# First block: VectorE takes the modulation rows and the attention step between the heads' sums of squares and the heads' scaling and finish

## The chip, the cores and the metric

The program runs on one core of a Trainium2 chip. The metric is the device time of one launch in microseconds (us), the median of the timed runs. The engines are named as in the profile: PE (TensorE), DVE (VectorE), ACT (ScalarE), POOL (GpSimd), and SP, whose queue carries the weight transfers.

## The reference, cut to what matters

Two transformer-like blocks run one after the other on 256 tokens of width 1024. The change touches the input projections of the first block, which has two layers:

```python
for l in range(DEPTH):                       # DEPTH = 2
    sh, sc, gt = jnp.split(jax.nn.silu(c) @ w_ada[l] + b_ada[l], 3, axis=-1)   # modulation rows; also for c_ctx
    h  = rms_norm(x, norm_g[l]) * (1 + sc[:, None]) + sh[:, None]
    hc = rms_norm(ctx, norm_g[l]) * (1 + sc_c) + sh_c
    qa, ka, va, ga, qb, kb, vb, gb, qn, kn, vn, gn = split_proj(h @ w_in[l])   # and the same of hc
    qa = axial_rope(rms_norm(qa.reshape(b, s, A_HEADS, 2, A_DK), diff_q_norm[l]), row, col)   # "heads": per-head
    qn = rms_norm(qn.reshape(b, s, C_HEADS, HEAD_DIM), nat_q_norm[l])                         # norm, some with rope
    ...
    oa = ...  (p[:, :, 0] - lam * p[:, :, 1]) @ v      # A: differential attention, 4 heads
    yb = gqa_attend(qb, kb_all, vb_all)                # B: grouped queries, 6 heads
    yn = neighbourhood_attend(qn, kn, ...)             # C: windowed attention with a bias table, 6 heads
    x = x + gt[:, None] * (jnp.concatenate([ya, yb, yn], axis=-1) @ w_out[l])
```

The change alters the order of some VectorE instructions and no value that is computed.

## The kernel before, in words

Tokens and context make four tiles of 128 rows (two of tokens, two of context). A projection is a run of chunks of 512 output columns; a chunk is four pieces, and a piece is two of the eight 128-row blocks of the contraction. The input projection of layer 0 is called in0, that of layer 1 in1; each has seven chunks. Below, (c, n) is piece n of chunk c.

Each weight piece is loaded by the SP queue into one of three raw buffers, split by ACT into a high part (L1093) and by DVE into a low part (L1685), and multiplied by PE three times (L739 to L741). In in0 DVE also works through the modulation weights beside each piece: four products (L1702, L1705) of one modulation piece. When four are done, PE sums them over the partitions (L666 for the column form, L673 for the gate rows) into bank 6 (gate rows: banks 6 and 7), and DVE adds the bias and stores them: `ada_keep`, L1713 and L1719 for columns, L1726 for gate rows. That falls at (2,0), (3,0), (4,0), (5,0) and (6,0) of in0. Layer 1's projection has no such work.

The heads of chunks 0, 2, 4 and 5 are normalised one chunk later, beside the pieces of the next chunk, so in chunks 1, 3, 5 and 6. At piece n the loop calls `process_in` with stage n + 2: ACT squares the heads of tile n + 2 (L1194), DVE sums the squares (`sum_squares`, L1822), POOL makes the reciprocal root (L1493, L1495), DVE scales tile n + 1 (`scale`, L1830), and DVE applies gain and rope to tile n (`finish`, L1848, L1853), for which POOL makes the rope's second product (L519). Tiles 0 and 1 are summed, and tile 0 is scaled, at the end of the chunk before. PE then turns a finished tile (L759): tile 0 in the middle and tile 1 at the end of piece 2, tile 2 in the middle and tile 3 at the end of piece 3.

From (2,1) on, one step of attention runs beside each piece. On PE a step is: the scores of the next unit, or of the next two (L863), the turn of the probabilities of the unit before (L873, into bank 6), and the attention product of the one before that (L888, into bank 7). On ACT: copy the turned probabilities (L1282), exponentials (L1273), for A heads a sum of squares of the output (L1293). On DVE: maxima of the new scores (L1901), weights of the current unit (L1912 to L1918, or L1926), and the output (L1936).

All engines run their instructions strictly in the order in which the program issues them and wait on semaphores. A bank of PSUM is taken again only when its last user has released it: bank 6 passes from modulation sums to turned probabilities when `ada_keep` has read it, the score banks 4 and 5 when the exponentials have read them. The order on DVE beside a piece was: heads (sum, scale, finish), `ada_keep`, attention step, the low part of the piece four ahead (L1685), modulation products. The next transfer of a weight piece waits until L1685 has read its raw buffer.

Of the kernel before, what the change touches and what calls it, by code (L numbers as in the profile page):

```python
# [64 lines left out]
def tiles_of(ph):  # L65
    return ALL_TILES if ph in ("in0", "out0", "in1") else X_TILES
# [164 lines left out]
def first_then_second_block(nc, a, out, known):  # L231
# [11 lines left out]
    with ExitStack() as ctx:  # L243
# [256 lines left out]
        for layer in range(2):  # L500
            n = 0
# [1176 lines left out]
        def _(dve):  # L1678
            at = [0]

            def split_until(n):
                for i in range(at[0], min(n, len(SPLITS))):
                    p = SPLITS[i]
                    dve.wait_ge(*weights_hi.seen(p))
                    dve.tensor_tensor(w_lo[:, i % SPLIT, :, :], raw[:, PIECE_AT[p] % RAW, :, :],  # L1685
                                      w_hi[:, i % SPLIT, :, :].bitcast(F32), ALU.subtract).then_inc(*weights_lo.at(p))
                at[0] = max(at[0], n)
# [97 lines left out]
            def project(ph, process, after_piece=None):  # L1785
                pairs = PROJ[ph][1] // 2
                limit = SPLIT_AT[(ph, 0, 0)] + PROJ[ph][0] * pairs if ph == "in0" else len(SPLITS)
                for c in range(PROJ[ph][0] - (1 if FOLLOWING.get(ph) and pairs <= SPLIT else 0)):
                    for n in range(pairs):
                        p = (ph, c, n)  # L1790
                        if ph in FOLLOWING and c == PROJ[ph][0] - 1 and n >= pairs - SPLIT:
                            continue
                        if after_piece:
                            after_piece((p, 0))
                        if ph in ("in0", "in1"):
                            process(ph, c - 1, (n + 2,))
                        if p in ADA_READY:
                            ada_keep(*ADA_READY[p])
                        if after_piece:
                            after_piece((p, 1))  # L1800
                        if n < pairs - 1:
                            split_until(min(limit, SPLIT_AT[p] + SPLIT + 1))
                        if p in ADA_BESIDE:
                            ada_products(ADA_BESIDE[p])
                        if n == pairs - 1:
                            split_until(min(limit, SPLIT_AT[p] + SPLIT + (1 if ph in FOLLOWING else 0)))
                            process(ph, c)
                            split_until(min(limit, SPLIT_AT[p] + SPLIT + 1))

            def process_in(ph, c, stages=(0, 1)):  # L1810


                if c not in CHUNK_HEADS:
# [4 lines left out]
                def sum_squares(tt):  # L1818
                    u = (ph, c, tt)
                    lo, w = head_span(*u)  # L1820
                    dve.wait_ge(*head_sq.seen(u))
                    dve.tensor_reduce(ss_of(tt % 2, w // d), sq[:, lo:lo + w].rearrange("p (n d) -> p n d", d=d), AX, ALU.add) \  # L1822
                        .then_inc(*head_sum.at(u))
# [31 lines left out]

                tts = tiles_of(ph)
                for k in stages:
                    if k < len(tts):
                        sum_squares(tts[k])
                    if 1 <= k <= len(tts):  # L1860
                        scale(tts[k - 1])
                    if k >= 2:
                        finish(tts[k - 2])

            def out_tile(ph, c, tt):
# [184 lines left out]
            project_with("in1", process_in, attention1(1))  # L2050
            y_part("out1", X_TILES[-1], 1)
            project("out1", process_out)
            end_of("out1", out_tile)

# [183 lines left out]
```

## Time and profile before

| | us |
|---|---|
| timed runs, median of 3 | 1259.74 |
| lowest and highest | 1258.07, 1260.96 |
| profiled execution, its own time | 1252.77 |
| its span | 1250.9 |
| PE busy in the span | 1137.0 (91%) |
| DVE busy | 727.0 (58%) |
| ACT busy | 598.6 (48%) |
| POOL busy | 256.8 (21%) |

The trace is of the profiled execution, whose time lies 7 us under the median of the timed ones; 1.9 us of it lie outside the span. In0 runs from about 28 to 290 us of the span, in1 from about 435 to 632 us. Times in the rows are microseconds from the start of the span. A row of a timeline merges neighbouring instructions of one kind; its second number runs from the first start to the last end, and in brackets stands the idle time of the engine before it and what ended that.

### The profile page before, as it was taken

What the parts mean: (1) busy time and instruction counts of PE and PEld (TensorE: products, weight loads), DVE (VectorE), ACT (ScalarE), POOL (GpSimd) and SP (SyncE); (2) the same over time, 40 slices, a digit from 0 to 9 for tenths busy, and PEclk for the clock granted to TensorE, in tenths of its full rate; (3) what the DMA queues carried; (4) which work ended last, traced back from release to release, by engine and by line L of the source; (5) the groups of instructions that cost most, each with busy time, mean ns of one, the idle gap of its engine ahead of it and who ended that gap; (6) DMA issues with size and microseconds to landing.
All of it is one profiled execution on the core that took longest, in us unless ns stands there. A gap on an engine that the chain in (4) does not pass through costs nothing.

```text
span 1250.9 us, 16717 instructions
## 1 busy us (share of the span) xinstructions
PE 1137.0 (91%) x5877; PEld 905.5 (72%) x5877; DVE 727.0 (58%) x1330; ACT 598.6 (48%) x1170; POOL 256.8 (21%) x324
## 2 busy tenths in 40 slices
PE   5978799898989878999989898999699999999997
PEld 2666578676668766777867686888588887888785
DVE  3467777777763744644455666565566646565543
ACT  3433453435762444554474454445444455454552
POOL 1482330354005221302300203000122101121100
PEclk8989899899999998899999899999999999999999
DMA  9755364323122322222202765555356665444301
GB/s 333 146 160 183 102 148 135 113 90 122 48 68 73 100 68 84 68 71 82 71 32 68 264 199 160 157 175 180 126 178 182 185 186 151 121 131 119 118 2 51
DMA packets 79290, 157.94 MB, mean 126 GB/s; under 512 B 5792, under 2 KB 6088, under 8 KB 78952
## 3 DMA queue, kind: packets, MB, share of 16 engines
q1 hardware_dynamic: 75880, 147.41, 38.0%
q0 software_dynamic: 3328, 9.46, 3.3%
q8 instruction: 49, 0.80, 0.3%
q14 instruction: 33, 0.27, 0.1%
HBM read 153.73 MB, written 3.11 MB: 125 GB/s over the span
## 4 chain that ended last, share of the span: by engine, by line
PE 71%; DVE 11%; ACT 6%; POOL 5%; issue 4%; DMA 2%; SPq 0%; ACTq 0%; POOLq 0%; DVEq 0%
PE bank L739 17%; PE bank L741 16%; PE bank L740 16%; PE bank L888 5%; PE bank L863 3%; PE bank L873 3%; POOL small L1495 3%; PE bank L966 2%; DVE work L1705 2%; DVE w_lo L1685 2%; PE bank L939 2%; PE bank L951 2%; ACT w_hi L1093 1%; PE bank L759 1%; POOL stage L519 1%
## 5 line engine op out<-in xcount | busy, mean ns | idle before, releaser
L739 PE MATMUL bank<-w_lo,h_hi 128*128 128x512 f32 (+1 forms) x1152 | 462.3, 401 | 27.7 <-DVE h_lo L1754 11.8
L741 PE MATMUL bank<-w_hi,h_hi 128*128 128x512 f32 (+1 forms) x1152 | 447.5, 388 | 0.0
L740 PE MATMUL bank<-w_hi,h_lo 128*128 128x512 f32 (+1 forms) x1152 | 447.1, 388 | 0.0
L1685 DVE TENSOR_TENSOR w_lo<-raw,w_hi 128x1024 fp32r<-128x1024 f32 x224 | 286.7, 1286 | 176.0 <-ACT w_hi L1093 174.5
L1093 ACT ACTIVATE w_hi<-raw 128x1024 fp32r<-128x1024 f32 x224 | 235.8, 1057 | 277.4 <-PE bank L741 237.8
L739 PEld LDWEIGHTS bank<-w_lo,h_hi 128*128 128x128 f32 x1152 | 222.6, 193 | 77.7 <-issue 29.7
L741 PEld LDWEIGHTS bank<-w_hi,h_hi 128*128 128x128 f32 x1152 | 221.7, 192 | 44.9
L740 PEld LDWEIGHTS bank<-w_hi,h_lo 128*128 128x128 f32 x1152 | 222.7, 193 | 39.5 <-issue 0.2
L888 PE MATMUL bank<-work,stage 128*128 128x128 f32 x640 | 94.4, 290 | 0.0
L1673 POOL TENSOR_TENSOR stage<-stage 128x512 f32<-128x512 f32 x24 | 42.3, 1784 | 218.0 <-DVE stage L519 218.0
L888 PEld LDWEIGHTS bank<-work,stage 128*128 128x128 f32 x640 | 85.5, 205 | 1.0 <-issue 0.2
L1282 ACT ACTIVATE stage<-bank 128x512 f32<-128x512 f32 (+1 forms) x96 | 50.2, 523 | 72.1 <-PE bank L873 71.9
L873 PEld LDWEIGHTS bank<-ident,stage 128*128 128x128 f32 x320 | 37.0, 147 | 65.3 <-issue 48.5
L1901 DVE TENSOR_REDUCE small<-bank 128x1 f32<-128x512 f32 (+1 forms) x96 | 53.2, 573 | 51.1 <-PE bank L863 51.1
L873 PE MATMUL bank<-ident,stage 128*128 128x128 f32 x320 | 56.9, 295 | 27.3 <-DVE work L1726 8.0
L1493 POOL TENSOR_SCALAR small<-small 128x1 f32<-128x1 f32 (+4 forms) x56 | 21.6, 386 | 268.1 <-DVE small L1822 222.7
L1495 POOL TENSOR_TENSOR small<-small 128x1 f32<-128x1 f32 (+4 forms) x56 | 73.3, 1308 | 4.7
L863 PE MATMUL bank<-work 64*128 64x512 f32 (+3 forms) x240 | 65.0, 582 | 8.6 <-ACT stage L1273 8.6
L1705 DVE SCALAR_TENSOR_TENSOR work<-raw,cvec,work 128x512 f32<-128x512 f32 x98 | 71.7, 781 | 1.2 <-DMA raw<-in_w_ada_dram 0.9
L1936 DVE SCALAR_TENSOR_TENSOR work<-bank,small,work 128x64 f32<-128x64 f32 x96 | 27.0, 282 | 70.8 <-PE bank L888 48.0
L1273 ACT ACTIVATE stage<-bank,small 128x512 f32<-128x512 f32 (+1 forms) x96 | 56.8, 596 | 19.8 <-DVE small L1901 19.5
L1210 ACT ACTIVATE work<-bank 128x512 f32<-128x512 f32 (+2 forms) x56 | 29.9, 534 | 55.8 <-PE bank L759 55.7
(173 smaller groups left out, 1090.7 us busy)
## 6 DMA issues: line engine op xcount, KB each, us to landing
raw<-in_b_w_in_dram SPq DMA_DIRECT2D x80, 512.0 KB, 3.7
raw<-in_w_in_dram SPq DMA_DIRECT2D x56, 512.0 KB, 4.1
raw<-in_a_w_in_dram SPq DMA_DIRECT2D x48, 512.0 KB, 4.3
raw<-in_w_ada_dram SPq DMA_DIRECT2D x32, 512.0 KB, 3.7
work<-in_w_ada_dram SPq DMA_DIRECT2D x16, 512.0 KB, 11.4
raw<-in_w_out_dram SPq DMA_DIRECT2D x16, 512.0 KB, 3.5
raw<-in_a_w_out_dram SPq DMA_DIRECT2D x16, 512.0 KB, 3.6
raw<-in_b_w_out_dram SPq DMA_DIRECT2D x8, 512.0 KB, 3.5
```

The costliest lines, as they stand in the source:

```text
L739: pe.matmul(bank, hT(h_hi, ph, at, tt), w_lo[:, s, k, lo:lo + w], start=first, stop=False)
L740: pe.matmul(bank, hT(h_lo, ph, at, tt), w_hi[:, s, k, lo:lo + w], start=False, stop=False)
L741: mm = pe.matmul(bank, hT(h_hi, ph, at, tt), w_hi[:, s, k, lo:lo + w], start=False, stop=last)
L863: mm = pe.matmul(bank[:, k0:512], qkT[base:base + d, tq, qt * P:(qt + 1) * P], qkT[base:base + d, tk, k0:512], start=True, stop=True)
L873: mm = pe.transpose(bank[:, j * P:(j + 1) * P], probs[prob_slot(layer, u, 0)][:, j * P:(j + 1) * P], ident[:, :])
L888: mm = pe.matmul(bank[:, 0:P], pT[i % 2][:, j * P:(j + 1) * P], vals[:, j, vcol:vcol + P], start=(j == kt0), stop=(j == 3))
L1093: act.activation(w_hi[:, i % SPLIT, :, :], raw[:, PIECE_AT[p] % RAW, :, :], ACT.Copy) \
L1273: act.activation(probs[slot][:, k0:512], bank[:, k0:512], ACT.Exp, bias=nm_col(u, m), accum_out=zc[0]).then_inc(*exps.at((layer, n)))
L1495: pool.tensor_tensor(out_ap, out_ap, half.broadcast_to([P, n]), ALU.pow).then_inc(*done.at(key))
L1685: dve.tensor_tensor(w_lo[:, i % SPLIT, :, :], raw[:, PIECE_AT[p] % RAW, :, :], w_hi[:, i % SPLIT, :, :].bitcast(F32), ALU.subtract).then_i ...
L1705: dve.scalar_tensor_tensor(to, w, c, to, ALU.mult, ALU.add).then_inc(*ada_vector.at((*p, k, who)))
L1901: dve.tensor_reduce(nm_col(u, m), bank[:, k0:512], AX, ALU.max, negate=True).then_inc(*row_max.at((u, m)))
```

## The change

At pieces 0 to 2 of chunks 1, 3, 5 and 6 of in0 and in1, DVE now does only the heads' sums of squares before `ada_keep` and the attention step, and the heads' scaling and finish after them, ahead of the low part of the next piece. At piece 3 of a chunk the order is as before. In chunk 1 there is neither a step nor an `ada_keep`, so nothing moves there. Nine places in each projection change their order. PE, ACT, POOL and SP issue the same instructions in the same order.

```diff
                         if after_piece:
                             after_piece((p, 0))
-                        if ph in ("in0", "in1"):
-                            process(ph, c - 1, (n + 2,))
+                        first_block = ph in ("in0", "in1")
+                        if first_block:
+                            process(ph, c - 1, (n + 2,), ("sum",) if n < pairs - 1 else ("sum", "finish"))
                         if p in ADA_READY:
                             ada_keep(*ADA_READY[p])
                         if after_piece:
                             after_piece((p, 1))
+                        if first_block and n < pairs - 1:
+                            process(ph, c - 1, (n + 2,), ("finish",))
                         if n < pairs - 1:
                             split_until(min(limit, SPLIT_AT[p] + SPLIT + 1))
...
-            def process_in(ph, c, stages=(0, 1)):
+            def process_in(ph, c, stages=(0, 1), parts=("sum", "finish")):
...
                 for k in stages:
-                    if k < len(tts):
+                    if k < len(tts) and "sum" in parts:
                         sum_squares(tts[k])
-                    if 1 <= k <= len(tts):
+                    if 1 <= k <= len(tts) and "finish" in parts:
                         scale(tts[k - 1])
-                    if k >= 2:
+                    if k >= 2 and "finish" in parts:
                         finish(tts[k - 2])
```

DVE at (3,0) of in0, before the change: the heads' sum (L1822), scale (L1830) and finish (L1848, L1853), then the two gate rows (L1726), then the attention step (L1901 to L1936).

```order
L1822 TENSOR_REDUCE small<-stage 128x8
L1830 TENSOR_TENSOR stage<-stage,small 128x512
L1848 TENSOR_TENSOR stage<-stage,tabs 128x384
L1848 TENSOR_TENSOR stage<-stage,tabs 128x128
L1853 TENSOR_TENSOR stage<-stage 128x512
L1726 TENSOR_TENSOR work<-work,bank 128x512 x2
L1901 TENSOR_REDUCE small<-bank 128x1 x2
L1912 RECIPROCAL small<-small 128x2
L1915 TENSOR_SCALAR small<-small 128x1
L1918 SCALAR_TENSOR_TENSOR stage<-stage,small 128x512
L1936 SCALAR_TENSOR_TENSOR work<-bank,small,work 128x64
L1685 TENSOR_TENSOR w_lo<-raw,w_hi 128x1024
```

The same place with the change (lines from L1811 on are numbered 3 higher in it, so L1825 is the sum, L1833 the scale, L1851 and L1856 the finish, L1904 to L1939 the step).

```order
L1825 TENSOR_REDUCE small<-stage 128x8
L1726 TENSOR_TENSOR work<-work,bank 128x512 x2
L1904 TENSOR_REDUCE small<-bank 128x1 x2
L1915 RECIPROCAL small<-small 128x2
L1918 TENSOR_SCALAR small<-small 128x1
L1921 SCALAR_TENSOR_TENSOR stage<-stage,small 128x512
L1939 SCALAR_TENSOR_TENSOR work<-bank,small,work 128x64
L1833 TENSOR_TENSOR stage<-stage,small 128x512
L1851 TENSOR_TENSOR stage<-stage,tabs 128x384
L1851 TENSOR_TENSOR stage<-stage,tabs 128x128
L1856 TENSOR_TENSOR stage<-stage 128x512
L1685 TENSOR_TENSOR w_lo<-raw,w_hi 128x1024
```

The four instructions of scale and finish have gone from ahead of the gate rows and the step to behind them. At (5,0) and (6,0) it is the same with L1713 (and L1719) in the place of L1726.

DVE at (3,0) of in1 with the change, where there are no modulation rows: the maxima of the scores now follow the heads' sum at once.

```order
L1825 TENSOR_REDUCE small<-stage 128x2
L1904 TENSOR_REDUCE small<-bank 128x1 x2
L1915 RECIPROCAL small<-small 128x2
L1918 TENSOR_SCALAR small<-small 128x1
L1921 SCALAR_TENSOR_TENSOR stage<-stage,small 128x512
L1939 SCALAR_TENSOR_TENSOR work<-bank,small,work 128x64
L1833 TENSOR_TENSOR stage<-stage,small 128x512
L1851 TENSOR_TENSOR stage<-stage,tabs 128x384
L1851 TENSOR_TENSOR stage<-stage,tabs 128x128
L1856 TENSOR_TENSOR stage<-stage 128x512
```

Before, the last four of these rows stood between the first and the second.

## Rows read from the trace of the kernel before

**Rows 1.** The page, busy time and share of the span by engine.

```profile
PE 1137.0 (91%) x5877; PEld 905.5 (72%) x5877; DVE 727.0 (58%) x1330; ACT 598.6 (48%) x1170; POOL 256.8 (21%) x324
```

**Rows 2.** Waits of PE, 130 to 640 us: total, times, longest.

```profile
PE bank L863 <- ACT stage L1273: 6.4, 4, 2.5
...
PE bank L873 <- DVE ada_cols L1713: 5.2, 2, 4.0
```

**Rows 3.** Timeline of PE in in0: start, length, work, idle before.

```profile
142.62 1.13 PE L863 MATMUL bank<-work 32*128 32x512 f32 x4
150.54 1.09 PE L873 MATMUL bank<-ident,stage 128*128 128x128 f32 x4 [6.79 <-DVE work L1726]
...
178.04 0.66 PE L759 MATMUL bank<-ident,stage 128*128 128x128 f32 x4 [0.30 <-DVE stage L1848]
```

**Rows 4.** Timeline of DVE at (3,0) of in0.

```profile
144.32 0.68 DVE L1822 TENSOR_REDUCE small<-stage 128x8 f32<-128x512 f32 x1
147.71 0.69 DVE L1830 TENSOR_TENSOR stage<-stage,small 128x512 f32<-128x512 f32 x1 [2.71 <-POOL small L1495]
...
149.71 1.28 DVE L1726 TENSOR_TENSOR work<-work,bank 128x512 f32<-128x512 f32 x2
...
153.98 0.28 DVE L1936 SCALAR_TENSOR_TENSOR work<-bank,small,work 128x64 f32<-128x64 f32 x1 [0.63 <-ACT bank L1293]
```

**Rows 5.** Waits of DVE, 144 to 178 us (chunk 3 of in0).

```profile
DVE work L1936 <- ACT bank L1293: 1.9, 3, 0.8
DVE small L1901 <- PE bank L863: 1.7, 2, 1.0
```

**Rows 6.** Windows: PE, PEld, DVE, ACT, POOL busy, granted clock, DMA.

```profile
144.00:146.00 2.00, 0.00 (x0) 0.00 (x0) 1.00 (x2) 0.00 (x0) 1.87 (x3) 0.86 0.28 23
```

**Rows 7.** Timeline of DVE at (5,0) of in0.

```profile
223.33 0.68 DVE L1822 TENSOR_REDUCE small<-stage 128x8 f32<-128x512 f32 x1
...
226.23 0.15 DVE L1713 TENSOR_TENSOR ada_cols<-bank,cols 128x8 f32<-128x8 f32 x1
```

**Rows 8.** Waits of DVE, 223 to 251 us (chunk 5 of in0).

```profile
DVE work L1936 <- ACT bank L1293: 2.5, 3, 1.2
DVE small L1901 <- PE bank L863: 1.7, 2, 1.2
DVE stage L1830 <- POOL small L1495: 0.9, 1, 0.9
```

**Rows 9.** Timeline of POOL, the bias mask of layer 0.

```profile
269.03 7.71 POOL L1552 TENSOR_TENSOR work<-work,win_mask 128x384 f32<-128x384 f32 x6
```

**Rows 10.** Timeline of DVE beside it, pieces 1 and 2 of chunk 6.

```profile
267.18 0.41 DVE L1830 TENSOR_TENSOR stage<-stage,small 128x256 f32<-128x256 f32 x1
...
275.81 1.21 DVE L1830 TENSOR_TENSOR stage<-stage,small 128x256 f32<-128x256 f32 x1
```

**Rows 11.** Timeline of DVE in chunk 3 of in1.

```profile
517.33 0.28 DVE L1822 TENSOR_REDUCE small<-stage 128x2 f32<-128x128 f32 x1
520.73 0.69 DVE L1830 TENSOR_TENSOR stage<-stage,small 128x512 f32<-128x512 f32 x1 [3.12 <-POOL small L1495]
...
522.74 1.28 DVE L1901 TENSOR_REDUCE small<-bank 128x1 f32<-128x512 f32 x2
...
536.61 1.29 DVE L1901 TENSOR_REDUCE small<-bank 128x1 f32<-128x512 f32 x2 [3.84 <-PE bank L863]
```

**Rows 12.** Timeline of PE in chunk 3 of in1.

```profile
524.28 2.74 PE L863 MATMUL bank<-work 32*128 32x512 f32 x4 [2.46 <-ACT stage L1273]
...
534.92 0.60 PE L759 MATMUL bank<-ident,stage 128*128 128x128 f32 x4
```

**Rows 13.** Windows over the same stretch, columns as in rows 6.

```profile
524.00:526.00 2.00, 1.72 (x4) 0.98 (x4) 1.83 (x6) 2.00 (x8) 1.57 (x3) 0.58 0.01 4
526.00:528.00 2.00, 2.00 (x8) 1.05 (x6) 1.97 (x6) 0.34 (x1) 0.94 (x2) 0.50 0.14 14
528.00:536.00 8.00, 8.00 (x45) 6.90 (x43) 4.60 (x10) 3.75 (x9) 0.39 (x1) 0.80 0.44 129
```

## The prediction

> **What bounds the kernel now.** I read the page first: PE is busy for 1137 us, 91% of the span [rows 1], so what counts is what makes PE wait, and DVE matters where PE waits for it. The second view is the waits of PE over the two stretches that the change touches. They name L873, the turn of the probabilities, waiting for `ada_keep`'s column form L1713 (5.2 us in two places, 4.0 and 1.2) and L863, the scores, waiting for exponentials (6.4 us in four places, the longest 2.5) [rows 2]. The timeline of PE has the largest one: at (3,0) of in0 PE ends its scores at 143.75 (142.62 + 1.13) and stands for 6.79 us until the gate rows L1726 have released bank 6 [rows 3]. The third view is DVE's timeline at that place. DVE ended the sum L1822 at 145.0, then waited 2.71 us for POOL's reciprocal root, then scaled and finished (2.00 us, 147.71 to 149.71), and only then read the bank that PE wanted [rows 4]. So the wait of PE is DVE's queue, and inside it POOL's time. At (5,0) the sum ends at 224.0 and L1713 starts at 226.23 [rows 7]. In in1, at (3,0), the sum ends at 517.6, DVE waits 3.12 us for POOL, and the maxima L1901 start at 522.74; the exponentials that need them hold PE's next scores back by 2.46 us, until 524.28 [rows 11, 12].
>
> The granted clock is the fourth view. In the stretch 144 to 146, with PE at rest since 143.75, it fell from 2.4 to 1.2 GHz (mean 0.86) [rows 6]. Round the stall of in1 it is 0.58, 0.50 and 0.80 of full in stretches of 2, 2 and 8 us [rows 13]. With f the mean, 2(1 - f) of a stretch lies at the lower level: 1.7 + 2.0 + 3.2 = 6.9 us.
>
> **The change, part by part.** No instruction is added or removed; on DVE nine groups in each projection change places. The sum is against the profiled execution, 1252.77 us (span 1250.9 and 1.9 outside).
>
> Chunk 3 of in0. L1726 can start at 145.0. Before, PE went on 0.83 us after L1726's start (149.71 to 150.54), so now at 145.8: the stall is 2.1 instead of 6.8 us, PE gains 4.7. DVE does not gain as much. Gate rows, maxima and weights took 153.98 - 149.71 - 0.63 = 3.64 us, so DVE reaches its output L1936 at 148.6; L1936 needs ACT's sum of squares, which comes a fixed chain after PE goes on (150.54 to 153.98, 3.44), at 149.3. POOL's root was there at 147.7, so scale and finish follow at once and end at 149.3 + 0.2 + 2.0 = 151.5, where before the low part started at 154.2: DVE gains 2.7, just the POOL wait. From there on, the two meet at the turns of the heads. DVE's other waits in this chunk are 1.9 (L1936, three) and 1.7 (L1901, two, for PE's scores) [rows 5]. Because PE is ahead now and scale and finish no longer stand before L1901, the 1.7 goes if the clock is up when (3,1) is multiplied, and none of it goes if PE stays at the lower level as long as before. So DVE finishes tile 3, for which PE waited already at 178.04 [rows 3], by 2.7 to 2.7 + 1.7 + 0.3 = 4.7 us earlier. I take 4.4, since PE now rests 2.1 and not 6.8 us. Bounds: 2.7 and, if the clock gives PE another 1.0 and DVE follows, 5.7.
>
> Chunk 5 of in0. L1713 starts at 224.0 instead of 226.2, PE gains 2.2. DVE's waits here sum to 2.5 + 1.7 + 0.9 = 5.1 [rows 8]; the 0.9 on POOL goes, and of the wait for scores some 0.5, because at (5,1) PE is 2.2 ahead and DVE 0.9. That makes 1.4 at the turn of tile 3. Bounds 0.9 (only the POOL wait) and 2.9 (the 2.2 and clock).
>
> Chunk 6 of in0. PE's wait of 1.2 goes. What covers the moved work is thin: at (6,1) scale and finish (0.41 each, as the row at 267.18) ran before POOL began the bias mask at 269.03; now they stand behind L1936, inside the mask's 7.7 us, where such a scale took 1.21 [rows 9, 10]. Two of them cost DVE 1.6 more, and tile 2 is finished behind (6,2)'s L1936, about when PE wants to turn it. I keep 0.4 of the 1.2. Bounds -0.8 and 1.2.
>
> Chunk 3 of in1. The maxima start at 517.6 instead of 522.74, 5.1 earlier. The exponentials and so PE's release would come at 524.28 - 5.1 = 519.2, before PE asks (521.8), so the 2.46 go whole. With no rest there, the 6.9 us at 1.2 GHz need not come: half of it, 3.4, is given back. That is 5.9. DVE is no bound: at (3,2) it waited 3.84 us for PE's scores [rows 11]. The turn of tile 1, at 534.92 before [rows 12], would be at 529.0; its finish, behind (3,1)'s L1936, I put at 528.4 (maxima at 523.9, 2.7 for the step, 0.2 and 1.4 for scale and finish, 0.2 between them), so it just fits. I take 5.8. Bounds 2.7 (DVE's gain at (3,0), if PE follows DVE) and 6.4.
>
> POOL's root is what this rests on in in1: it came at 520.7, and DVE would want it at 520.3. A rule speaks against the change here: by the Trainium skill, SBUF — State Buffer, section "SBUF: two separate sides", a GpSimd instruction and a DVE instruction with two SBUF inputs lock the port pair that they share, and the later one is blocked for the whole instruction. The trace agrees in kind (1.21 against 0.41 [rows 9, 10]). The root's long instruction now runs beside the weights of the step, one of which has two SBUF inputs, instead of an idle DVE; by the rule the root comes up to one such instruction later, and the sum would be some 0.7 smaller.
>
> Chunks 5 and 6 of in1 (six places): PE waited for none of this before, and the moved heads (0.4 to 1.4 us) are wanted by PE's turns microseconds later: nothing. The low part L1685 comes later by the moved heads wherever DVE did not gain; it is for a piece that PE reaches four pieces on, and the transfer behind it has the same cover: nothing, and if the cover failed, up to 1.3 us at a place.
>
> Sum: 4.4 + 1.4 + 0.4 + 5.8 = 12.0. The profiled execution would take 1240.8. The timed runs lay 7.0 us higher, in no place that this trace shows; I carry the offset over: 1259.7 - 12.0 = 1247.7.
>
> **The rivals.** First, the turns follow DVE: PE gets its banks early but then waits for heads that are finished behind an L1936, so that each chunk gives the lower bound, 2.7 + 0.9 - 0.8 + 2.7 = 5.5: 1254.2. For it: PE waits for tile 3 at 178.04 even now. Against: DVE idles 6.3 us in that chunk, and 3.8 at one place of in1.
>
> Second, the clock helps everywhere: 5.7 + 2.9 + 1.2 + 6.4 = 16.2: 1243.5. For it: shorter rests. Against: the clock fell in 144 to 146, while PE would still rest in the new order until 145.8, and the same holds at (5,0).
>
> Third, the change doesn't do what it says: PE at L873 waited for something else, and the bank was only last by the profile. Then nothing moves: 1259.7. Against: PE goes on within a microsecond of L1726 in one place, and of L1713 in another.
>
> Fourth, slower: heads behind the step. The heads of tiles 1 and 2 are now finished only after an L1936 that itself waits for PE and ACT, in six chunks: twelve turns. A group of heads takes 0.4 to 2.0 us, on average about 1.3. If PE waited that long at all twelve, it would lose 15.6 against the 12.0: 3.6 slower, 1263.3. It decides from about nine or ten waited turns on. Against: my placing of the first four has waits of 0 to 0.5 us.
>
> **How the numbers follow.** Forecast 0.60; turns follow DVE 0.18; clock everywhere 0.10; nothing 0.06; slower 0.06. I call 0.2% (2.5 us) what a measurement can tell. Faster holds the first three, 0.88; same 0.06; slower 0.06. The range reaches from the sum of the upper bounds with half a microsecond of spread, 1243.0, to beyond the first rival, 1256.0; what is left out is mainly the last two cases.
>
> **What would show it.** Right: L873's idle at (3,0) of in0 is 2 us, not 6.8, at (5,0) under 2 and not 4.0; no wait of L1833 (the scale) for POOL at (3,0); in in1 L863 at (3,1) waits for nothing and the clock stays at 1.0 there. At the end of chunk 3 of in0 PE is 4 to 5 us ahead, at the end of in0 about 6, at the end of in1 about 12. Wrong: new waits of L759 for L1851 of over 1 us, a clock that falls in in1's chunk 3 all the same, or gains that are gone by the start of the next phase.

## The result, and the profile after

| | before | with the change |
|---|---|---|
| timed runs, median (us) | 1260.35 (1258.07 to 1261.09, 4 runs) | 1240.52 (1236.3 to 1243.42, 4 runs) |
| ratio, 95% interval | | 0.9846 [0.9825, 0.9867] |
| profiled execution, own time | 1252.77 | 1242.56 |
| its span | 1250.9 | 1240.8 |

The change makes the kernel 1.5% faster: 19.8 us, where 12.0 were forecast and the range ended at 1243.0. The two profiled executions differ by only 10.1 us in span. That of before lay 7.6 us under the median of the timed runs of before in this table (7.0 under that of the first three, which the prediction had); the one with the change lies 2.0 us over its own. So most of what the forecast missed is not in this pair of traces, and the experiments had to find it.

First the busy times of the changed kernel, as in [rows 1].

```profile
PE 1134.9 (91%) x5877; PEld 900.9 (73%) x5877; DVE 729.6 (59%) x1330; ACT 599.3 (48%) x1170; POOL 253.8 (20%) x324
```

Busy times hardly move; what goes is idle time of PE and some slow multiplying. The waits of PE, 130 to 640 us (total, times, longest), answer to [rows 2]:

```profile
PE bank L759 <- DVE stage L1851: 3.2, 5, 1.0
...
PE bank L873 <- DVE work L1726: 3.2, 2, 2.0
PE bank L863 <- ACT stage L1273: 3.1, 2, 2.2
PE bank L873 <- DVE ada_cols L1713: 1.7, 1, 1.7
```

L873 waits 1.7 instead of 5.2 us for the column form, and 3.2 instead of 8.0 for the gate rows. The scores lost two of their four waits, the longest (2.5) and one of 0.8 at the end of in1. New is the first row: five turns of heads wait 3.2 us for a finish that now stands behind the step. Before, L1848 made one turn wait, for 0.3 us [rows 3]; the waits of two other turns for L1853, in in1, are there before and after (5.4 and 5.5 us).

Timeline of PE in in0 (start, length, work, idle before), the answer to [rows 3]; the last two rows are the turns of tiles 2 and 3 of chunk 3:

```profile
144.40 1.13 PE L863 MATMUL bank<-work 32*128 32x512 f32 x4
147.53 0.63 PE L873 MATMUL bank<-ident,stage 128*128 128x128 f32 x4 [2.00 <-DVE work L1726]
...
171.24 0.66 PE L759 MATMUL bank<-ident,stage 128*128 128x128 f32 x4 [0.33 <-DVE stage L1851]
...
175.69 0.66 PE L759 MATMUL bank<-ident,stage 128*128 128x128 f32 x4 [1.03 <-DVE stage L1851]
```

Timeline of DVE at the same place, (3,0) of in0, the answer to [rows 4]:

```profile
146.11 0.68 DVE L1825 TENSOR_REDUCE small<-stage 128x8 f32<-128x512 f32 x1
146.70 1.28 DVE L1726 TENSOR_TENSOR work<-work,bank 128x512 f32<-128x512 f32 x2
...
149.60 0.75 DVE L1921 SCALAR_TENSOR_TENSOR stage<-stage,small 128x512 f32<-128x512 f32 x1
150.51 0.28 DVE L1939 SCALAR_TENSOR_TENSOR work<-bank,small,work 128x64 f32<-128x64 f32 x1 [0.16 <-ACT bank L1293]
150.71 0.68 DVE L1833 TENSOR_TENSOR stage<-stage,small 128x512 f32<-128x512 f32 x1
```

The gate rows start as the sum ends, the 2.71 us wait for POOL is gone (the scale at 150.71 has no bracket), and the output L1939 waits 0.16 us. At (5,0) and in chunk 6, PE's rows are these (the last two are turns of tiles 2 and 3 in chunk 6):

```profile
223.44 0.41 PE L873 MATMUL bank<-ident,stage 128*128 128x128 f32 x2 [1.75 <-DVE ada_cols L1713]
...
248.73 0.66 PE L759 MATMUL bank<-ident,stage 128*128 128x128 f32 x4 [1.04 <-DVE stage L1851]
...
277.19 0.44 PE L759 MATMUL bank<-ident,stage 128*128 128x128 f32 x2 [0.18 <-DVE stage L1851]
...
281.01 0.44 PE L759 MATMUL bank<-ident,stage 128*128 128x128 f32 x2 [0.62 <-DVE stage L1851]
```

In in1, DVE at (3,0) and PE's scores at (3,1) answer to [rows 11, 12], and the window (PE, PEld, DVE, ACT, POOL busy, granted clock, DMA) to [rows 13]:

```profile
513.81 0.28 DVE L1825 TENSOR_REDUCE small<-stage 128x2 f32<-128x128 f32 x1
514.00 1.28 DVE L1904 TENSOR_REDUCE small<-bank 128x1 f32<-128x512 f32 x2
...
517.22 0.69 DVE L1833 TENSOR_TENSOR stage<-stage,small 128x512 f32<-128x512 f32 x1 [0.38 <-POOL small L1495]
```

```profile
518.26 1.13 PE L863 MATMUL bank<-work 32*128 32x512 f32 x4
```

```profile
518.00:526.00 8.00, 8.00 (x53) 6.42 (x54) 7.76 (x16) 4.41 (x10) 4.05 (x6) 1.00 0.21 66
```

The maxima follow the sum at once, the scores wait for nothing, and PE stays at 2.4 GHz through the stretch that ran at means of 0.58, 0.50 and 0.80 before. The four matmuls of the scores take 1.13 us there instead of 2.74.

### The profile page after: what moved, and what is told of

The parts are those of the page before. It is cut to its first block, busy times and chain, and to the rows that moved or that the text cites. A ratio compares the mean times of both kernels' runs of the same rounds, so it can differ in the third digit from the quotient of the medians.

```text
span 1240.8 us, 16717 instructions
## 1 busy us (share of the span) xinstructions
PE 1134.9 (91%) x5877; PEld 900.9 (73%) x5877; DVE 729.6 (59%) x1330; ACT 599.3 (48%) x1170; POOL 253.8 (20%) x324
## 3 DMA queue, kind: packets, MB, share of 16 engines
q1 hardware_dynamic: 75880, 147.41, 37.5%
## 4 chain that ended last, share of the span: by engine, by line
PE 60%; DVE 7%; ACT 5%; issue 3%; POOL 2%; DMA 1%; POOLq 0%; ACTq 0%; DVEq 0%; SPq 0%
PE bank L739 14%; PE bank L741 14%; PE bank L740 14%; PE bank L888 4%; PE bank L966 2%; PE bank L873 2%; PE bank L863 2%; PE bank L939 2%; PE bank L951 2%; ACT w_hi L1093 1%; DVE w_lo L1685 1%; PE bank L759 1%; DVE work L1705 1%; POOL small L1495 1%; PE bank L720 1%
## 5 line engine op out<-in xcount | busy, mean ns | idle before, releaser
L739 PE MATMUL bank<-w_lo,h_hi 128*128 128x512 f32 (+1 forms) x1152 | 462.7, 402 | 27.7 <-DVE h_lo L1754 11.8
L739 PEld LDWEIGHTS bank<-w_lo,h_hi 128*128 128x128 f32 x1152 | 222.3, 193 | 78.3 <-issue 30.6
L888 PE MATMUL bank<-work,stage 128*128 128x128 f32 x640 | 91.3, 283 | 0.0
L1904 DVE TENSOR_REDUCE small<-bank 128x1 f32<-128x512 f32 (+1 forms) x96 | 53.3, 574 | 51.4 <-PE bank L863 51.3
L888 PEld LDWEIGHTS bank<-work,stage 128*128 128x128 f32 x640 | 82.0, 198 | 1.2 <-issue 0.4
L873 PEld LDWEIGHTS bank<-ident,stage 128*128 128x128 f32 x320 | 36.1, 145 | 56.9 <-issue 41.7
L1495 POOL TENSOR_TENSOR small<-small 128x1 f32<-128x1 f32 (+4 forms) x56 | 73.5, 1312 | 4.7
L873 PE MATMUL bank<-ident,stage 128*128 128x128 f32 x320 | 55.3, 288 | 18.7 <-DVE h_lo L1782 6.1
L1493 POOL TENSOR_SCALAR small<-small 128x1 f32<-128x1 f32 (+4 forms) x56 | 16.1, 287 | 259.6 <-DVE small L1825 215.8
L1939 DVE SCALAR_TENSOR_TENSOR work<-bank,small,work 128x64 f32<-128x64 f32 x96 | 27.1, 282 | 71.5 <-PE bank L888 49.4
```

The lines of the kernel that those rows point to most:

```text
L739: pe.matmul(bank, hT(h_hi, ph, at, tt), w_lo[:, s, k, lo:lo + w], start=first, stop=False)
L873: mm = pe.transpose(bank[:, j * P:(j + 1) * P], probs[prob_slot(layer, u, 0)][:, j * P:(j + 1) * P], ident[:, :])
L888: mm = pe.matmul(bank[:, 0:P], pT[i % 2][:, j * P:(j + 1) * P], vals[:, j, vcol:vcol + P], start=(j == kt0), stop=(j == 3))
L1495: pool.tensor_tensor(out_ap, out_ap, half.broadcast_to([P, n]), ALU.pow).then_inc(*done.at(key))
L1904: dve.tensor_reduce(nm_col(u, m), bank[:, k0:512], AX, ALU.max, negate=True).then_inc(*row_max.at((u, m)))
```

## The experiments

All are the kernel before with one rule for the "late" order, that is, scaling and finish behind the step. The core of the edit is this, and the experiments differ in the line that sets `late`; the versions that treat the modulation rows otherwise show their own edit below.

```diff
-                            process(ph, c - 1, (n + 2,))
+                            process(ph, c - 1, (n + 2,), ("sum",) if late else ("sum", "finish"))
...
+                        if late:
+                            process(ph, c - 1, (n + 2,), ("finish",))
```

| kernel | late at | median us (range, runs) | before on the same chip | ratio [95%] |
|---|---|---|---|---|
| change, once more | 18 places | 1241.08 (1238.38 to 1244.25, 6) | 1258.3 | 0.9876 [0.9849, 0.9903] |
| change, a third time | 18 places | 1242.09 (1239.76 to 1244.35, 5) | 1258.47 | 0.9875 [0.9856, 0.9895] |
| before, again | none | 1259.12 (1251.93 to 1260.83, 12) | 1258.3 | 1.0005 [0.9984, 1.0025] |
| in0 only | 9 places | 1251.55 (1248.05 to 1254.16, 12) | 1258.3 | 0.9952 [0.9934, 0.9971] |
| in1 only | 9 places | 1250.12 (1246.15 to 1253.27, 11) | 1258.3 | 0.9941 [0.992, 0.9961] |
| chunk 3 of in0 | 3 places | 1250.28 (1247.47 to 1257.42, 8) | 1259.46 | 0.9941 [0.9918, 0.9965] |
| chunk 6 of in0 | 3 places | 1256.49 (1252.02 to 1259.58, 12) | 1259.46 | 0.998 [0.9966, 0.9994] |
| first places | 4 places | 1239.81 (1237.46 to 1243.08, 4) | 1259.46 | 0.9846 [0.9826, 0.9866] |
| first places, again | 4 places | 1237.75 (1237.35 to 1243.6, 5) | 1258.47 | 0.9852 [0.9827, 0.9877] |
| first places, third | 4 places | 1242.02 (1238.29 to 1243.6, 4) | 1259.63 | 0.9856 [0.9839, 0.9872] |
| modulation rows first | in0, rows alone | 1247.78 (1241.31 to 1250.39, 6) | 1259.46 | 0.9898 [0.987, 0.9927] |
| the same and (3,0) of in1 | | 1238.46 (1237.9 to 1240.76, 4) | 1258.47 | 0.9844 [0.9825, 0.9864] |
| rows ahead of the sum too | 4 places | 1239.66 (1238.91 to 1242.48, 6) | 1258.3 | 0.9856 [0.9833, 0.9879] |
| first places, chunk 3 of in1 | 6 places | 1240.16 (1237.55 to 1242.78, 5) | 1259.63 | 0.9843 [0.9825, 0.9861] |

**Where the time went: six traced executions of before and three of the change.** Both kernels were run again unchanged, to see whether the 7 us missing from the first trace lie in stretches that the change touches (a term was too small) or elsewhere. The further profiled executions of before took 1254.91, 1258.28, 1255.16, 1258.53 and 1260.91 us against the 1252.77 of the first.

> The kernel before once more, for a second trace and the spread of its times. Theory A (the terms of the sum were right, the profiled execution that they were set against was a lucky one): its trace shows PE's wait of about 6.8, 4.0 and 1.2 us in in0 and 2.5 us in in1 again, but a time of 1258 to 1261, and the 5 to 8 us above 1252.8 lie in stretches that the change does not touch, as more time at the lower clock. Theory B (a term was undersized): the same places cost more than in the first trace, by 5 us or more together.

> The changed kernel once more. Theory A: 1236 to 1243, and against the kernel before, landmark by landmark, 6 us by the end of in0 and 12 by the end of in1 once the stretches at the lower clock are taken off; the rest of the 20 us is clock. Theory B: against a trace of before with a usual time, 8 us or more in either projection at an equal clock.

> The kernel before, for one more trace. Its two traces so far are of runs at 1252.8 and 1254.9, and its timed runs have their median at 1258 to 1259. Theory C (a slow spell of the clock that the changed places bring on in most runs of before, and not in those two): a run of 1257 or more shows spells at the lower clock in in0 or in1, at or right behind PE's rests, that the first trace has not. Theory A: the extra time lies in stretches that the change does not touch (0 to 122, 310 to 500, past 700 us).

> As the look before it, another execution: theory C, the extra 5 us of a usual run lie between 122 and 310 or 500 and 700 us; theory A, elsewhere.

> As the two looks before it, another execution: theory C, the extra 5 us of a usual run lie between 122 and 310 or 500 and 700 us; theory A, elsewhere.

> The kernel before, a further trace. Usual case by the traces so far: 163.6 us between 122 and 310, 200.0 between 500 and 700. If the run is at 1259 or more, the theory that the missing 2 to 3 us are lost at touched places wants more than 163.6 or 200.0 there; the rival has them in 310 to 500 or past 700.

> The changed kernel, beside its four-place version on one chip, for a third trace. If the clock spell that the first traces of it show at (4,0) in one of two comes about half the time, its times spread over 4 us or more, 1238 to 1243. Median 1240 to 1241.5.

The table cuts the span at the same matmuls (L739) of PE in every trace. The names of its rows are round; in the first trace the cuts lie at 122.3, 181.8, 219.4, 257.9, 282.6, 500.2, 540.3, 626.1 and 700.4 us. Low is time at 1.2 GHz, added up from the granted clock.

| stretch, us | before, first trace | before, mean of 6 | change, first trace | change, mean of 3 | gain, first pair | gain, means |
|---|---|---|---|---|---|---|
| to 122 | 122.3 | 123.1 | 123.1 | 123.6 | -0.8 | -0.6 |
| 122 to 182, chunk 3 | 59.5 | 59.5 | 56.4 | 55.7 | 3.1 | 3.8 |
| 182 to 222, chunk 4 | 37.6 | 37.6 | 39.1 | 37.0 | -1.5 | 0.6 |
| 222 to 258, chunk 5 | 38.5 | 38.7 | 37.1 | 37.5 | 1.4 | 1.2 |
| 258 to 310, chunk 6 on | 24.7 | 26.8 | 23.9 | 23.9 | 0.8 | 2.9 |
| 310 to 500 | 217.6 | 218.9 | 216.9 | 218.4 | 0.7 | 0.5 |
| 500 to 540, chunk 3 of in1 | 40.1 | 39.9 | 34.2 | 34.1 | 5.9 | 5.9 |
| 540 to 640 | 85.8 | 85.8 | 85.8 | 85.8 | 0 | 0 |
| 640 to 700, end of in1 and after | 74.3 | 74.2 | 73.7 | 73.4 | 0.6 | 0.8 |
| 700 to the end | 550.5 | 550.3 | 550.6 | 549.8 | -0.1 | 0.5 |
| span | 1250.9 | 1254.9 | 1240.8 | 1239.4 | 10.1 | 15.5 |
| low | 91.7 | 99.6 | 78.1 | 77.3 | | |

The means give 15.5 us. The ratios of the second and third timings give 15.6 and 15.7 (0.0124 of 1258.3 and 0.0125 of 1258.5), the first 19.4; the intervals of the three overlap. Over all timings on record the medians are 1259.1 for before (92 runs) and 1241.9 for the change (15 runs), 17.2 apart. The change's third timing, 1242.09, lies 0.6 us over what was expected of it.

Of the two theories on the first trace each held for about half: the other five traces of before are 4.7 us longer, 2.5 of it in chunk 6, which the change touches, and the rest mainly where it changes nothing (1.5 between 310 and 500, 0.9 ahead of 122). The slowest traced execution, 1260.91 us, has 163.6 us between 122 and 310 and 199.9 between 500 and 700, no more than the usual trace; its extra time lies between 310 and 500 (220.6 us) and ahead of 122. So what separates the slowest runs of before from its traces' mean was not lost, in that run, at places that the change touches.

The row that the first trace hid is chunk 6. PE rests at (6,0) for 1.2 us before the change; in five of the six traces, not in the first, the clock fell there. Windows of the first trace of before (columns as above):

```profile
260.00:264.00 4.00, 2.83 (x17) 1.92 (x17) 3.33 (x10) 0.91 (x3) 3.12 (x3) 1.00 0.47 132
264.00:268.00 4.00, 4.00 (x19) 3.28 (x18) 3.67 (x10) 0.74 (x5) 0.63 (x1) 1.00 0.37 137
268.00:272.00 4.00, 4.00 (x22) 3.35 (x21) 1.92 (x5) 1.35 (x5) 3.94 (x4) 1.00 0.46 129
```

and of another execution of the same program:

```profile
260.00:264.00 4.00, 2.84 (x22) 2.03 (x21) 2.90 (x8) 0.79 (x2) 3.67 (x5) 0.88 0.21 28
264.00:268.00 4.00, 4.00 (x13) 3.42 (x14) 3.35 (x9) 1.65 (x6) 0.58 (x1) 0.50 0.65 234
268.00:272.00 4.00, 4.00 (x15) 3.16 (x14) 2.14 (x6) 0.00 (x0) 3.03 (x4) 0.77 0.44 131
```

PE is busy for as long in both (2.83 and 2.84 us, then all of it), but gets through 41 matmuls in the last two windows of the first and through 28 in those of the other. 2(1 - f) of each gives 1.0 + 4.0 + 1.8 = 6.8 us at 1.2 GHz, for which the stretch took 27.5 instead of 24.7 us.

**Chunk 6 alone** tests that by itself, by `late = (ph, c) == ("in0", 6) and n < pairs - 1`.

> The new order in chunk 6 of in0 only. The forecast's term for it was 0.4 us (1.2 of PE's wait less 0.8 for heads inside POOL's mask). Theory A: 0 to 1 us. Theory C (the second trace of before had a spell of 6.8 us at the lower clock from (6,0) on, which the first one had not): the wait there often brings such a spell, the change takes it away, and the mean gain is 2 to 4 us.

It gained 0.2% [0.06, 0.34], 2.5 us, against 0.4 forecast. Its trace has no rest at (6,0) and no fall of the clock:

```profile
262.96 0.44 PE L873 MATMUL bank<-ident,stage 128*128 128x128 f32 x2
```

```profile
264.00:268.00 4.00, 4.00 (x19) 3.31 (x18) 3.67 (x10) 1.17 (x5) 0.56 (x1) 1.00 0.68 251
```

Its stretch took 23.9 us, 2.9 under the mean of before. In twelve traces of kernels that take the modulation rows early at (6,0), the clock never fell between 258 and 310; in the eight others, with the rest of 1.2 us, it fell in five (it held in the first trace and in those of the chunk 3 and the in1 version). So what goes at (6,0) is a rest of 1.2 us that in most executions also costs 1.3 to 2.8 us of slow multiplying. Why it spares some executions no row shows.

**The halves**, `late = ph == "in0" and n < pairs - 1`, and the same with in1:

> The change in in0 alone (in1 in the order of before). Forecast terms: 4.4 + 1.4 + 0.4 = 6.2 us faster than before. Theory A: 6 us, or up to 10 if clock luck differs. Theory B: 10 or more here or in the in1-only kernel. The two partial gains should add up to the whole change's (about 20 as timed) if the projections are independent.

> The change in in1 alone. Forecast term: 5.8 us faster than before. Theory A: 6 us. Theory B: 8 to 12 us, since the stall there may often cost more time at the lower clock than it did in the first trace.

In0 is worth 0.48% [0.29, 0.66], 6.0 us, and in1 0.59% [0.39, 0.8], 7.4 us, at before's 1258.3. The forecast had 6.2 and 5.8. Together they make 13.4 against the whole's 15.6 to 19.4, which their intervals of some 2.5 us to each side allow. The in0 version's runs fall into two groups, six at 1248.1 to 1250.1 and six at 1253.0 to 1254.2; its traced one (1253.37) is of the upper group and has a slow spell at (4,0) and 23.9 us of low clock between 310 and 500 us, where the change's traces had 13.0 to 20.3.

**Chunk 3 of in0 alone**, `late = (ph, c) == ("in0", 3) and n < pairs - 1`:

> The new order in chunk 3 of in0 only. The forecast's term was 4.4 us; the traces with the change gave 2.4, 2.4 and 4.9 for the stretch from (2,1) to the end of (4,0), depending on whether the clock fell once more at (4,0). Theory A: 3 to 5 us faster than before. Theory C: the chip's clock takes part of it back behind the place, and it gives 2 to 3.

0.59% [0.35, 0.82], 7.4 us, is more than the 4.4 of its term. In its trace the stretch 122 to 182 fell to 55.7 (3.8 under the mean of before) and the next, 182 to 222, from 37.6 to 36.0, since the clock no longer fell at (4,0). These 5.4 us lie inside the interval. In the change's own first trace the clock did fall there. Windows of that one,

```profile
188.00:192.00 4.00, 4.00 (x18) 3.71 (x17) 2.55 (x7) 1.91 (x7) 0.00 (x0) 0.50 0.60 230
```

and of the second execution of the same program:

```profile
188.00:192.00 4.00, 4.00 (x21) 3.32 (x20) 3.44 (x6) 1.18 (x6) 0.00 (x0) 1.00 0.57 181
```

One such spell is the 3.1 us between 39.1 and 36.0 in that stretch.

**Which places pay.** The first-places version has `late = (ph == "in0" and n == 0) or (ph, c, n) == ("in1", 3, 0)`.

> The new order only at piece 0 of chunks 3, 5 and 6 of in0 and at (3,0) of in1: the four places where PE waited on DVE's queue. Theory A (the wait at those four places is all that the change removes): as fast as the whole change, about 1241 here, or 1 to 2 us faster, since the heads of tiles 1 and 2 are finished earlier and PE's new waits of 1.0 us at the turn of tile 3 go in part. Theory B (the other fourteen places matter, because DVE no longer does heads while scores wait): 3 us or more slower than the whole change.

> The new order at the four places only, on the same chip as the whole change. Theory A (only these four places pay, the other fourteen cost PE 1 to 2 us in all at the turns of the heads): 1 to 3 us faster than the whole change. Rival (the other places are free): the same within 0.5 us.

Four places do what eighteen do. Its spans, 1236.6, 1235.8 and (third time, below) 1236.3, are 3.1 us under the change's mean. PE's rest at (3,0) is the same; the turn of tile 3 comes 31.0 us after the scores of (3,0) (143.40 to 174.39; 31.3 with the change), and tile 2 waits for nothing. PE in its second trace:

```profile
146.52 0.79 PE L873 MATMUL bank<-ident,stage 128*128 128x128 f32 x4 [1.99 <-DVE work L1726]
...
174.39 0.66 PE L759 MATMUL bank<-ident,stage 128*128 128x128 f32 x4 [1.40 <-DVE stage L1851]
```

At (5,0) the rest is the same too, but no turn of chunk 5 or 6 waits for a finish (one of 0.37 us in chunk 6 in the third trace): 222 to 258 took 35.7 to 35.8 us (37.0 to 38.4 with the change), 258 to 310 took 23.5 (23.9). So the places at n = 1 and 2 cost the change 1.2 us or more in chunk 5 and 0.4 in chunk 6. In the timed runs the 3 us do not show: over all timings the change has a median of 1241.9 (15 runs) and this version 1241.0 (13 runs), both from 1236 or 1237 to 1244. The traced executions were among its fastest; what the others do is not in a trace.

**The bank alone.** Here only the modulation rows go ahead of scaling and finish, and the step stays behind them; `keep` is true at the five places with modulation rows, of which (3,0), (5,0) and (6,0) have heads:

```diff
-                            process(ph, c - 1, (n + 2,))
+                            process(ph, c - 1, (n + 2,), ("sum",) if keep else ("sum", "finish"))
                         if p in ADA_READY:
                             ada_keep(*ADA_READY[p])
+                            process(ph, c - 1, (n + 2,), ("finish",))
```

> In in0 only, modulation rows go ahead of the heads' scale and finish, and the attention step stays behind them; in1 as before. Theory A (in in0 the release of bank 6 is what counts): PE's rests at (3,0), (5,0), (6,0) are 2.0, 1.8 and 0 us as in the whole change, and the time is that of the in0-only kernel within 2 us (6 to 7 under before). Theory B (the step's maxima matter as well): under 4 us of gain.

1.02% [0.73, 1.3], 12.8 us, with in0 alone: more than the 6.0 of the late order at nine places of in0, by 6.8 us where 2 at most were expected. The traces agree: the four stretches from 122 to 310 took 162.6 us before in the mean, 156.3 in the in0 version (6.3 less) and 150.1 here (12.5 less), as in the first-places version (150.2 to 150.6). Of the 6.2 us between the two versions 3.1 are the slow spell at (4,0), which two of the four traces with the late order in all of in0 have; against the trace of the change with the same time at 1.2 GHz in chunks 4 and 5, 152.5 us, 2.4 remain. So in in0 the release of bank 6 is all that pays: to move the step ahead as well adds nothing at its places, and the places without modulation rows lose. With (3,0) of in1 late as well (`keep or (ph, c, n) == ("in1", 3, 0)`, there behind the step):

> In in0 only the modulation rows go ahead of the heads' scale and finish (the step stays behind them); in in1 the new order at (3,0). If the release of bank 6 is all that matters in in0, it is as fast as the four-place kernel within 1 us, 1239 to 1241. If the maxima going ahead matters in in0 as well, it is 2 us or more slower.

The median is 1238.46, with all four runs under 1241. It is 3.6 us under that of the change beside it on the same chip, with intervals of the ratios that overlap slightly ([0.9825, 0.9864] and [0.9856, 0.9895]).

**The sum of squares too.** The first-places version with the modulation rows ahead of the heads' sum as well:

```diff
+                        if p in ADA_READY:
+                            ada_keep(*ADA_READY[p])
                         if ph in ("in0", "in1"):
                             process(ph, c - 1, (n + 2,), ("sum",) if late else ("sum", "finish"))
-                        if p in ADA_READY:
-                            ada_keep(*ADA_READY[p])
```

> A version meant to be the fastest: the new order only at the four places of the first-places kernel, and there the modulation rows go ahead of the heads' sum as well. PE's rests at (3,0) and (5,0) of in0 should shrink from 2.0 and 1.7 us to 1.4 and 1.1. Theory A: 1.0 to 1.5 us faster than the first-places kernel (1238.5 at its 1239.8). Rival: the sum now comes 0.6 to 1.2 us later, POOL's root with it, and at (3,0) the scale waits for POOL again, so that DVE loses what PE gains: same time.

PE in that trace, (3,0) and the turn of tile 3:

```profile
146.84 0.63 PE L873 MATMUL bank<-ident,stage 128*128 128x128 f32 x4 [1.40 <-DVE work L1726]
...
175.03 0.66 PE L759 MATMUL bank<-ident,stage 128*128 128x128 f32 x4 [2.91 <-DVE stage L1851]
```

The rest fell by 0.6 and the turn's wait grew by 1.5: PE gets the bank earlier and then stands for heads that are later. The clock held behind the rest of 1.4 us (mean 1.00 from 142 to 154) and fell behind the turn instead (0.57 from 176 to 180). The stretch 122 to 182 took 57.4 us, 2.2 more than with the first places; the time stayed.

**Chunk 3 of in1.** With only (3,0) late there, PE had a new wait: the turn of tile 1 stood for ACT's copy of the turn before it. From the second trace of the first-places version:

```profile
522.61 0.63 PE L759 MATMUL bank<-ident,stage 128*128 128x128 f32 x4 [2.03 <-ACT work L1210]
```

In two other kernels with that rest (modulation rows first with (3,0) of in1, and rows ahead of the sum) the clock fell after it, and 500 to 540 took 39.4 and 39.0 us instead of 35.8. The change, late at (3,1) and (3,2) too, has no such rest: 34.1. The last version keeps these two places: `late = (ph == "in0" and n == 0) or ((ph, c) == ("in1", 3) and n < pairs - 1)`.

> The late order at piece 0 of chunks 3, 5 and 6 of in0 and at pieces 0 to 2 of chunk 3 of in1, six places. In the four-place version PE waited 2.0 us at the turn of tile 1 in chunk 3 of in1 for ACT's copy of an earlier turn (L1210), a wait that the change, with all three places late there, did not have. Theory A: that wait comes from the order at (3,1) of in1, so it goes here and the version is 1 to 2 us under the four-place one, about 1236.5; PE's stretch from 500 to 540 us of before falls from 35.8 to 34.1 us. Theory B: what it gains there it gives back in the stretch from 640 to 700 us, where the four-place version took 71.6 us and the change 73.1 to 73.7 (low clock 3.4 against 10.2 us): then it comes out at the four-place version's time, 1238 to 1239.

> The four-place version once more beside it on the same chip: 1237.5 to 1240, with 35.8 us from 500 to 540 and 71.6 from 640 to 700.

Both theories held in part. The turn stands at no wait,

```profile
523.16 0.60 PE L759 MATMUL bank<-ident,stage 128*128 128x128 f32 x4
```

and the stretch took 33.9 us, but 640 to 700 took 73.0 instead of 71.6 with 10.2 against 3.4 us of low clock: 1.9 gained, 1.4 given back. The medians, 1240.16 and 1242.02, do not tell the two apart, and 1242.02 lies above the 1240 that was expected at most.

## Why the prediction was wrong

**The bound and the mechanism were right, step by step.** PE's wait at (3,0) was DVE's queue with POOL's root in it: 2.00 us against "2.1 instead of 6.8", and 1.75 against 4.03 at (5,0). At (6,0) the 1.2 went. The scale at (3,0) finds its root waiting. In in1 the scores at (3,1) wait for nothing and the clock stays up. One sign that was to show the prediction wrong came too, just: new waits of L759 for L1851 of over 1 us (1.03 and 1.04). And the lead of PE was put at about 6 us at the end of in0 and 12 at the end of in1. In the first pair of traces it is 3.0 and 9.6, since a slow spell at (4,0) took 1.5 back and 0.8 was lost ahead of 122; in the means it is 7.9 and 14.2.

**Chunk 3 of in0, 4.4 forecast: right.** The turn of tile 3 came at 175.69, at 178.04 before [rows 3], and PE had come to the scores of (3,0) 1.78 us later (144.40 against 142.62): 2.35 + 1.78 = 4.1 us. The stretch gave 3.1 in the first pair, 3.8 in the means. DVE has the last word there, as forecast: two turns wait for the finish, 0.33 and 1.03 us.

**Chunk 5, 1.4 forecast: right,** with 1.4 and 1.2. The wait too: 2.2 gained at (5,0) and 1.4 left at the turn of tile 3 make a wait of 0.8 there, and it was 1.04. What the forecast did not ask is whether that wait was needed: the places at n = 1 and 2 gave back at least 1.2 us of what the four-place version has.

**Chunk 6, 0.4 forecast: mis-sized.** Where the clock stayed up before, it is 0.8. In the mean over the traces it is 2.9, and alone in timed runs 2.5 [0.8, 4.3]. Its step "Bounds -0.8 and 1.2" failed: the bounds price PE's rest of 1.2 us and not what follows it, because in the one trace at hand nothing followed. The same trace showed the clock fall in the rest at (3,0) [rows 6], so a spell like that belonged into the upper bound. The part that was priced in detail, two scales inside POOL's mask for 1.6 us of DVE, came out smaller: only the first ran beside the mask (0.74 us, and the finish behind it 1.24), the second took 0.56 behind its end, and the four scales and finishes of tiles 1 and 2 took 0.5 us longer than before. Two turns waited, 0.18 and 0.62 us.

**Chunk 3 of in1, 5.8 forecast: right,** with 5.9. Another 0.8 came in the stretch 640 to 700, where no time was forecast. No slow spell was saved there: the time at 1.2 GHz is 10.2 us before and with the change. What changed is where the spell at the end of in1 lies. Before, it came behind a wait of the scores for exponentials; with the change it begins some 4 us earlier and lies over the place of that wait, so that PE multiplies slowly where it stood. PE before, then with the change:

```profile
632.12 1.12 PE L863 MATMUL bank<-work 64*128 64x512 f32 x2 [0.83 <-ACT stage L1273]
```

```profile
621.08 3.54 PE L863 MATMUL bank<-work 64*128 64x512 f32 x4
```

**The port.** The root did not come later: it ended 3.4 us behind the start of the sum in both (513.81 to 517.19, and 517.33 to 520.69 before [rows 11]). In in1 it took 1.64 us, with the step's instruction of two SBUF inputs beside it for all of that instruction's length. POOL with the change, then POOL before:

```profile
515.55 1.64 POOL L1495 TENSOR_TENSOR small<-small 128x8 f32<-128x8 f32 x1
```

```profile
519.06 1.63 POOL L1495 TENSOR_TENSOR small<-small 128x8 f32<-128x8 f32 x1
```

The Trainium skill, SBUF — State Buffer, section "SBUF: two separate sides", would have one of the two blocked while the other runs; here neither was, and L1921 at 515.70 took 0.75 us, as it does at 149.60 with POOL's L1495 over by 149.46. The 0.7 us was not to be taken off.

**The step that failed first: the offset.** The four terms sum to 12.0, and in the first pair of traces their stretches gave 3.1 + 1.4 + 0.8 + 5.9 = 11.2 (10.1 with the rest of the span). Then the prediction said of the timed runs that they "lay 7.0 us higher, in no place that this trace shows; I carry the offset over". That takes it that none of the 7.0 lies in a stretch that the change touches. Over the traces the offset is much smaller: the six executions of before have a mean own time of 1256.8, 1.5 to 3.6 us under the medians of the timed runs, and the three of the change 1241.3, under 1 us from the median of all its timed runs. The first trace was a low one. Against it the other five were 4.7 us longer in span, of which 2.5 us in chunk 6 (27.2 against 24.7), beside a wait that the change removes.

So the miss of 7.2 us (1247.7 against 1240.5) has two halves. With the 15.5 us of the means in the place of 12.0 the forecast would have been 1244.2. Of these 3.5, chunk 6 is 2.5; 1.4 are the stretch at (4,0), with 1.1 us less at the lower clock, and the one at the end of in1, which no term counted; chunks 3 and 5 of in0 came out 0.8 smaller than forecast, and the stretches that the change does not touch differ by 0.4 in its favour. The other 3.7 lie between timings and traces: the 1259.7 from which the forecast subtracts is 3.0 over the mean of the six traced executions of before, and the change's first timing 0.8 under the mean of its three. The second and third timings, 15.6 and 15.7, do not have this difference. So scatter between executions would explain it, but no trace holds it, and the cause is not shown. The rival "clock helps everywhere", 1243.5, came nearest and had a chance of 0.10. It is not what happened: in the change's three traces a slow spell still follows the shorter rest at (3,0) and at (5,0), chunks 3 and 5 gave 3.8 and 1.2 and not that rival's 5.7 and 2.9, and in chunk 6 the clock gave more than any bound had. That the time came near it is luck.

**What stays open.** Why the clock holds after the rest at (6,0) in some executions and not in others; why runs of one kernel fall into groups some 5 us apart; where the 1.7 us lie by which all timings together (17.2) exceed the traces (15.5); whether the version with the modulation rows first beats the change by the 3 to 4 us that traces and medians suggest; and why the 3.1 us by which the first-places version leads in the traces are 0.9 in the timed runs.

## What to carry to other kernels

A rest of PE costs its own length and, in some executions, slow matmuls behind it; price both, and read more than one execution before a term is set near zero. Where timed runs lie off the profiled one, let the difference fall on the stretches that the change touches as well, and widen the range on that side by a spell for each rest removed. Put ahead of a wait what releases something that the bounding engine wants, and try each further place by itself: in in0 the moved step gained nothing and the places at n = 1 and 2 lost 1.2 us in chunk 5, while in chunk 3 of in1 the same two places gained 1.9.

## What the runs showed of the hardware

- The same program at the same place kept 2.4 GHz after a rest of 1.17 us in one execution and ran 6.8 us at 1.2 GHz in another, which cost 2.8 us. Six executions of before had 91.7 to 109.4 us at the lower clock in spans of 1250.9 to 1258.9 us; between 310 and 500 us, where PE's work was the same, 16.8 to 23.9 us.
- A shorter rest did not always save a spell, but it shortened it: in the eleven traces with 2.0 us of rest at (3,0) the stretch 122 to 182 had 3.4 to 5.4 us at the lower clock, in the eight with 6.8 us of it 7.6 to 10.6.
- POOL's L1495 and DVE's L1921 ran side by side at their usual 1.64 and 0.75 us. Beside POOL's mask L1552 (265.89 to 273.01 us with the change) a scale of 128x256 took 0.74 us, L1833 at 267.42, and 1.21 before, where 0.41 is usual. The one of 1.21 ended 0.28 us behind the mask (277.02 against 276.74 [rows 9, 10]), as one that had to wait for the mask's last instruction would.
